# The opening's w_ada product in column halves with its own ring slots, and the convolution's first gated rows rounded early

## The reference, cut to what matters

```python
mod = silu(c) @ w_ada + b_ada            # 9 vectors of 1024: shift, scale, gate of three places
sh1, sc1, gt1, ... = split(mod, 9)
u = rmsnorm(x, g_norm_ffn1) * (1 + sc1) + sh1
h = x + 0.5 * gt1 * (silu(u @ w_in[:, :2816]) * (u @ w_in[:, 2816:])) @ w_out
...                                      # attention and pooling, a second FFN, a last rmsnorm
b_gate, c_gate, h = split(x @ conv_w_in, 3)
y = (b_gate * causal_dwconv3(c_gate * h)) @ conv_w_out
x = layer_norm(ALPHA * x + y)
x = layer_norm(ALPHA * x + top-2-of-64-experts(x))      # expert weights: 3 MB each, all are loaded
...                                      # sparse attention, a second set of 64 experts
```

## Time and profile before

| | us |
|---|---|
| median of 3 runs | 2670.45 |
| lowest, highest | 2669.17, 2670.98 |
| profiled execution | 2668.95 |
| its span | 2667.0 |

### The profile page before, as it was taken

How to read it: one execution, slowest core, us unless ns; L and a number is a source line. 1 busy time by engine, 2 the same in 40 slices (tenths; PEclk the granted TensorE clock), 3 DMA queues, 4 the chain that set the end, 5 groups by cost and what they waited for, 6 DMA issues and landing times.

```text
span 2667.0 us, 38184 instructions
## 1 busy us (share of the span) xinstructions
PE 2425.0 (91%) x14539; PEld 1778.1 (67%) x14540; DVE 1352.8 (51%) x2767; ACT 860.5 (32%) x1484; POOL 215.5 (8%) x168
## 2 busy tenths in 40 slices
PE   6999999999999999999987888889989988888787
PEld 4888888877678888787754444447755865544454
DVE  5766645442552244544653444336955574444445
ACT  4222335565332224322322111124367341211122
POOL 1000003000000000000011111110036001111110
PEclk9999999999999999999999898899999989989899
DMA  8666422112432232222489999995220349999987
GB/s 287 212 196 196 165 87 89 63 49 79 142 111 95 94 118 101 81 95 95 171 359 422 422 422 422 422 401 193 80 95 21 145 195 421 422 422 422 422 336 303
DMA packets 201771, 591.62 MB, mean 222 GB/s; under 512 B 10512, under 2 KB 126432, under 8 KB 152784
## 3 DMA queue, kind: packets, MB, share of 16 engines
q1 hardware_dynamic: 198496, 575.47, 56.1%
q0 software_dynamic: 2896, 14.47, 1.7%
q10 hardware_dynamic: 288, 0.43, 0.1%
HBM read 588.17 MB, written 7.41 MB: 223 GB/s over the span
## 4 chain that ended last, share of the span: by engine, by line
PE 66%; DMA 22%; DVE 4%; ACT 3%; issue 2%; SPq 1%; POOL 1%; DVEq 0%; ACTq 0%; POOLq 0%
PE bank L2181 40%; DMA arena<-in_exp_w 19%; PE bank L2550 7%; PE bank L2274 5%; DMA ring<-in_exp_w 2%; PE bank L2573 1%; SPq L609 1%; PE bank L2438 1%; DMA ring<-in_w_ffn_in 1%; DVE ring_low L1351 1%; PE bank L2785 1%; PE bank L2361 1%; PE bank L2591 1%; PE bank L2519 1%; PE bank L2754 1%
## 5 line engine op out<-in xcount | busy, mean ns | idle before, releaser
L2181 PE MATMUL bank<-parts 128*128 128x512 f32 x2560 | 795.9, 392 | 10.9 <-DVE parts L1628 4.8
L2181 PEld LDWEIGHTS bank<-parts 128*128 128x128 f32 x2560 | 482.2, 189 | 112.4 <-DVE ring_low L1351 6.5
L2181 PE MATMUL bank<-parts,ring_low 128*128 128x512 f32 x1280 | 500.5, 391 | 0.0
L2550 PE MATMUL bank<-ring,arena 128*32 128x256 f32 x2112 | 303.8, 447 | 83.6 <-DMA arena<-in_exp_w 83.6
L1351 DVE TENSOR_TENSOR ring_low<-ring,parts 128x2048 fp32r<-128x2048 f32 x109 | 245.1, 2251 | 179.2 <-ACT parts L838 170.2
L2550 PE MATMUL bank<-arena 128*32 128x256 f32 x2112 | 304.0, 447 | 32.2 <-issue 25.5
L838 ACT ACTIVATE parts<-ring 128x2048 fp32r<-128x2048 f32 x109 | 204.4, 1879 | 227.7 <-DMA ring<-in_w_ffn_in 115.4
L2181 PEld LDWEIGHTS bank<-parts,ring_low 128*128 128x128 f32 x1280 | 241.8, 189 | 51.0
L765 POOL COPY arena<-U 128x2048 f32<-128x2048 f32 x60 | 112.6, 1907 | 1762.5 <-PE bank L2550 1043.9
L2550 PEld LDWEIGHTS bank<-ring,arena 128*32 128x32 f32 x2112 | 141.0, 124 | 158.5 <-issue 135.0
L2550 PEld LDWEIGHTS bank<-arena 128*32 128x32 f32 x2112 | 142.1, 124 | 82.8 <-issue 49.1
(11 more groups left out here) (380 smaller groups left out, 3587.8 us busy)
## 6 DMA issues: line engine op xcount, KB each, us to landing
ring<-in_exp_w SPq DMA_DIRECT2D x188, 1024.0 KB, 18.9
arena<-in_exp_w SPq DMA_DIRECT2D x132, 1024.0 KB, 18.6
U<-in_exp_w SPq DMA_DIRECT2D x60, 1024.0 KB, 23.1
ring<-in_w_ffn_in SPq DMA_DIRECT2D x44, 1024.0 KB, 5.6
ring<-in_w_ada SPq DMA_DIRECT2D x36, 1024.0 KB, 5.5
ring<-in_w_ffn_out SPq DMA_DIRECT2D x20, 1024.0 KB, 5.1
ring<-in_w_in SPq DMA_DIRECT2D x18, 1024.0 KB, 5.0
ring<-in_conv_w_in SPq DMA_DIRECT2D x12, 1024.0 KB, 5.1
```

The source lines that it names most:

```text
L2181: i = mm(o, a[:, cols[0], cols[1]], b, start=first_ and n == 0, stop=last_ and n == 2)
L2550: x = mm(bank[p][lanes_at:lanes_at + LANES, 0:2 * P].rearrange("p (w n) -> p w n", w=2), XW[:, k, LANES * (2 * p + e):LANES * (2 * p + e) ...
```

## The change

**Opening.** The eight w_ada chunks are cut as 512 rows by 512 columns, in the order scale and shift of columns 0 to 511, then scale and shift of 512 to 1023. Each group of two chunks gives half a vector. Only four chunks are loaded ahead of the first pair of FFN chunks, which has ring slots 4 and 5 for itself; the other four come behind it, then two more w_ada chunks, then the second pair (slots 2 and 3). VectorE, not ScalarE, copies the turned tiles of x. The first pair's chunks are split in two parts each (rows of tiles 0 to 3 and 4 to 7), and tiles 0 to 3 are made while the second half of the shift and scale is not yet known. `first_pair` multiplies A's two halves of the columns with tiles 0 to 3, then w_ada chunks 4 and 5, B's first half of the columns, chunks 6 and 7, B's second half, and then tiles 4 to 7. The turn of the layer norm's vectors moves behind the pair.

**Convolution.** `EARLY` is a pair of memories for the rounded first four row tiles. Its high part lies in `parts` 8192 to 10240 and its low part at 10240 to 12288, which is where `W13[0]` takes expert 0. The roundings of row tile d - 2 stand in steps 2 to 5, the output product reads its first chunk from there, and expert 0's W1 and W3 are loaded after the third use count of `conv_out`. The waits of TensorE for the end of the convolution move to the second half of the columns.

```diff
+        EARLY = (rounded(8192, 4, SEQ), rounded(10240, 4, SEQ))
...
-            return first["ffn0"] + (0 if c == 0 else 5 + 4 * (c - 1))
+            return first["ffn0"] + (0 if c == 0 else 8 if c == 1 else 5 + 4 * c)
...
-                    stream_a.append((flat(A["w_ada"], 2 * (a % 4), 2, D * (1 - a // 4), D), 2, D, "ada_mm", a + 1))
+                    stream_a.append((flat(A["w_ada"], 4 * (a % 2), 4, D * (1 - a // 2 % 2) + 512 * (a // 4), 512), 4, 512,
+                                     "ada_mm", a + 1))
...
-        ada_chunks(ADA_FIRST)
+        ada_chunks(4)
...
-                    ada_chunks(3 if c in (0, 10) else 2)
+                    ada_chunks({0: 6, 1: 3, 10: 3}.get(c, 2))
...
+            if n < ffn_at(0, 2):
+                return (0, 1, 2, 3, 4, 5, 0, 1, 2, 3, 0, 1, 2, 3, 0, 4, 5)[n]
             if n < first["mix"]:
-                return n % RING
+                return (n - ffn_at(0, 2)) % RING
...
-                sp.wait_ge(*((sem("ffn1_out_used"), 12), (sem("att_max"), ATT["max"] + 64))[layer])
-                for j in range(2):
-                    matrix(layer, j, 0, 0)
+                if layer:
+                    sp.wait_ge(sem("att_max"), ATT["max"] + 64)
+                    for j in range(2):
+                        matrix(layer, j, 0, 0)
...
                 for j in range(2):
                     matrix(layer, j, 3, 3)
+                if layer == 0:
+                    sp.wait_ge(sem("conv_out_used"), 3)
+                    for j in range(2):
+                        matrix(layer, j, 0, 0)
...
+                row(1)
+                first_high(0, 0)
+                act.wait_ge(sem("ada_mod"), 4)
+                tile(0)
+                tile(1)
+                first_high(1, 0)
+                tile(2)
+                tile(3)
+                first_high(0, 1)
+                first_high(1, 1)
+                row(2)
+                row(3)
+                act.wait_ge(sem("ada_mod"), ADA_FIRST)
+                for k in range(4, KT):
+                    tile(k)
...
+                if 2 <= d < 6:
+                    act.wait_ge(sem("conv_bc"), d - 1)
+                    tile_high(EARLY[0][:, d - 2], BC[:, d - 2])
...
+            dve.wait_ge(sem("ada_mm"), 2)
+            nc.vector.tensor_copy(AROW[:, 0], bank[4][:]).then_inc(sem("ada_row"), 1)
+            vector(0)
+            for k in range(KT):
+                dve.wait_ge(sem("x_tp"), k + 1)
+                nc.vector.tensor_copy(H[:, k], bank[k % 4][:]).then_inc(sem("x_h"), 1)
+                if k == 6:
+                    dve.wait_ge(sem("keep"), 16)
+                    roots(0)
+            dve.wait_ge(sem("x_h"), KT)
+            dve.wait_ge(sem("rstd"), 1)
+            normed(0)
+            vector(1)
+            first_low(0, 0)
+            rest_of(0)
+            normed(1)
+            rest_of(1)
+            normed(2)
+            first_low(1, 0)
+            rest_of(2)
+            normed(3)
+            rest_of(3)
+            first_low(0, 1)
+            first_low(1, 1)
+            vector(2)
+            for k in range(4, KT):
+                normed(k)
+            vector(3)
+            for k in range(4, KT):
+                rest_of(k)
             ffn(0)
...
+                if 2 <= d < 6:
+                    tile_low(tiles_at["conv_out"] + d - 2, EARLY, d - 2, BC[:, d - 2])
...
+            def first_pair():
+
+                def product(which, s, k):
+                    return passes(bank[2 * s + which][:], both(which), (k, slice(P * s, P * s + P)),
+                                  (UP[0][:, k], UP[1][:, k]), k == 0, k == KT - 1)
+
+                pe.wait_ge(sem("opening"), 2)
+                for k in range(4):
+                    pe.wait_ge(sem("t_low"), tiles_at["ffn0"] + k + 1)
+                    for s in range(2):
+                        product(0, s, k)
+                ada_rows(4)
+                ada_rows(5)
+                pe.wait_ge(sem("opening"), 3)
+                for k in range(4):
+                    product(1, 0, k)
+                    if k == 1:
+                        ada_sums(2)
+                ada_rows(6)
+                ada_rows(7)
+                for k in range(4):
+                    product(1, 1, k)
+                    if k == 1:
+                        ada_sums(3)
+                pe.wait_ge(sem("w_low"), 2)
+                for s in range(2):
+                    for k in range(4, KT):
+                        pe.wait_ge(sem("t_low"), tiles_at["ffn0"] + k + 1)
+                        for which in range(2):
+                            x = product(which, s, k)
...
+                    src = EARLY if name == "conv_out" and c == 0 else x
...
+                    if name == "conv_out" and (half, c) == (1, 0):
+                        pe.wait_ge(sem("conv_bc"), 8)
+                        pe.wait_ge(sem("side_out"), 9)
...
-            pe.wait_ge(sem("conv_bc"), 8)
-            pe.wait_ge(sem("side_out"), 9)
+            pe.wait_ge(sem("conv_bc"), 7)
+            pe.wait_ge(sem("conv_cg"), 8)
```

More of the change, by code:

```diff
@@ L400, in build @@
         first["ada"] = 0
-        ada_first = tuple(range(ADA_FIRST))
+        ada_first = tuple(a if a < 4 else a + 2 for a in range(ADA_FIRST))
         def ada_chunks(n):
@@ L903, in norm, with first_high, first_norm, row @@
                     tile_high(UM[0][:, KT - 1], U[:, KT - 1])
+            def first_high(i, part):
+                which, n = splits[i]
+                landed(act, which, n)
+                C = slice(CHUNK // 2 * part, CHUNK // 2 * part + CHUNK // 2)
+                made = A_(high(i)[0][:, C], ring[:, slots[which][n], C], ACT.Copy)
+                if part == 0:
+                    st.did(made)
+                else:
+                    made.then_inc(sem("w_high"), 1)
+            def first_norm():
+                act.wait_ge(sem("pool_step"), 4)
+                st.wait()
+                A_(small[:, 56:57], epsc[:, 0:1], ACT.Sqrt)
+                A_(small[:, 48:52], small[:, 60:64], ACT.Sqrt, scale=1.0 / D, bias=epsc[:, 0:1]).then_inc(sem("root"), 1)
+                def row(g):
+                    act.wait_ge(sem("ada_mm"), 2 * g + 2)
+                    if g >= 2:
+                        act.wait_ge(sem("ada_sum"), g - 1)
+                    evac(AROW[:, g % 2], bank[4 + g % 2][:], "ada_row")
+                def tile(k):
+                    act.wait_ge(sem("normed"), k + 1)
+                    A_(UP[0][:, k], U[:, k], ACT.Identity, bias=mod[:, k:k + 1]).then_inc(sem("t_high"), 1)
+                row(1)
[13 more added lines that the diff above has]
+                    tile(k)
             def ffn(i):
@@ L1600, in _ @@
             st.wait()
[L1601 to L1620, removed]
+            nc.vector.tensor_copy(CZ[:, :, 0:1], csil[:].unsqueeze(2)).then_inc(sem("opening"), 1)
+            def vector(g):
+                dve.wait_ge(sem("ada_sum"), g + 1)
+                c = KT * (1 - g % 2) + 4 * (g // 2)
+                TTn(mod[:, c:c + 4], bank[7][:, 4 * g:4 * g + 4], par[:, PC["b_ada"] + c:PC["b_ada"] + c + 4], ALU.add)\
+                    .then_inc(sem("ada_mod"), 2)
+                dve.wait_ge(sem("ada_mod"), 2 * g + 2)
+                if g % 2 == 0:
+                    C = slice(2 * g, 2 * g + 4)
+                    seq(STT(out=gains[:, C], in0=mod[:, c:c + 4], scalar=1.0, in1=par[:, PC["g_ffn1"] + 2 * g:PC["g_ffn1"] + 2 * g + 4],
+                            op0=ALU.add, op1=ALU.mult))
@@ L1621, in _, with first_low, normed @@
+            def first_low(i, part):
+                dve.wait_ge(*((sem("act_step"), TT + i + 1), (sem("w_high"), i + 1))[part])
+                n = slots["a"][splits[i][1]]
+                C = slice(CHUNK // 2 * part, CHUNK // 2 * part + CHUNK // 2)
+                TTn(ring_low[:, n, C], ring[:, n, C], high(i)[0][:, C].bitcast(F32), ALU.subtract)\
+                    .then_inc(sem(("opening", "w_low")[part]), 1)
+            def normed(k):
                 STT(out=U[:, k], in0=H[:, k], scalar=gains[:, k:k + 1], in1=bank[6][:],
@@ L1622, in _, with rest_of @@
                     op0=ALU.mult, op1=ALU.mult).then_inc(sem("normed"), 1)
[L1623 to L1626, removed]
+            def rest_of(k):
                 dve.wait_ge(sem("t_high"), tiles_at["ffn0"] + k + 1)
@@ L2156, in _ @@
             pe.wait_ge(sem("csil"), 1)
-            pe.wait_ge(sem("ada_cz"), 1)
+            pe.wait_ge(sem("opening"), 1)
             ada_rows(0)
             ada_rows(1)
+            ada_sums(0)
             pe.wait_ge(sem("x_in"), 16)
@@ L2193, in pair @@
                             pe.wait_ge(g, c * 2 + (base + s - 1))
-                        if s == 0 and it is None and r == 0 and i:
+                        if s == 0 and it is None and r == 0:
                             pe.wait_ge(sem("w_low"), s0 + 2)
                         if it is None and r == s == 0:
[L2197 to L2200, removed]
```

(6 more changed lines are left out.)

71 lines of the change are left out of this document (27 added, 44 removed).

## The result

| | before | after |
|---|---|---|
| median us (20 runs each, same chip) | 2667.39 | 2672.22 |
| lowest, highest | 2665.23, 2671.5 | 2668.32, 2674.68 |
| profiled execution, its span | 2668.95, 2667.0 | 2669.14, 2667.3 |

The ratio is 1.0016, with a 95% interval of 1.001 to 1.0022. The change makes the kernel 4.8 us slower, where 5.5 us faster was forecast. The difference lies under the 0.2% that the prediction took for the bound of what can be told, but 20 runs on each side resolve it.

What follows compares the result with a forecast made beforehand. It took TensorE, busy 91% of the span, as the bound, and VectorE's serial list as the opening's new one. Join 5.3 plus opening 0.2 gave 5.5 us: 2670.45 - 5.5 = 2664.9 us, range 2660.5 to 2668.5.

Steps and rivals of the forecast that it cites:

- the opening: Start of the kernel through the first FFN pairs: earlier TensorE start, later a new wait; 0.2 us won in all.
- the wait at 92 us: TensorE's wait of 1.2 us in the opening before; forecast to go because the second pair's chunks are loaded early.
- the join: Convolution's end to its output product: TensorE's 3.83 us without work goes, with the clock price behind it; 5.3 us won.
- the steps of the convolution: Steps 2 to 5, which take the moved roundings: cost 0, at worst 0.2 us for two tight steps.
- Rival (2): At the join, another wait replaces the roundings (second chunk or step 5): 2 to 3 us won, 2667 to 2668; chance 0.12.
- The matrices: First expert's two matrices (2 MiB), loaded later: cost 0, or 5.0 us if they stood in the path.
- Rival (3): The matrices reach the experts' first turn late because transfers share bandwidth; the 5.3 us are lost again, 2670; chance 0.08.
- The opening, up to TensorE's start: Kernel start to the first pair's first matrix product: TensorE starts at 28.4 us, 40.88 before.
- From there: Opening behind TensorE's start: VectorE's list delays the second B; with the wait at 92 us and clock, 0.2 us won.
- VectorE's list: Serial w_ada, low-part and gate work in the opening: starts at 49.7 us, takes 19.9, becomes the new bound.
- second B: First pair's second B in the opening: TensorE waits 5.5 us until 69.6, then loses 1.45 us to the clock.
- Rival (4): Opening: clock falls in TensorE's broken groups from 28 to 36 us and stays low; 3.0 us slower, 2673.5; chance 0.07.

Runs made afterwards that it cites:

- e1: The whole change with the first FFN's ring slots renamed from s to (s + 5) mod 6, nothing else: 2666.58 us, ratio 0.9994 to the kernel before.
- e2: The kernel before with the first FFN's ring slots turned from n mod 6 to (n + 1) mod 6, nothing else: 2676.49 us, ratio 1.0035.
- e3: The kernel before with only the convolution's part of the change (early roundings, later load of expert 0's matrices): 2662.65 us, ratio 0.9982.
- e5: e1 with VectorE doing the second B's low part and gate product ahead of w_ada chunk 10: 2659.57 us, ratio 0.9966 to the kernel before.
- e4: e1 without the convolution's part, so the opening alone with renamed slots: 2670.38 us, ratio 1.0011 to the kernel before.
- e6: e5 with GpSimd's small loads waiting for the eighth A chunk's use, not the second: 2657.6 us, ratio 0.9966 to the kernel before.
- e7: e1 with GpSimd's small loads waiting for the eighth A chunk's use, VectorE's order unchanged: 2666.31 us, ratio 0.999 to the kernel before.

## Why the prediction was wrong

**The step that failed** is a term that the prediction put at nothing without a reason: the stretch between the opening, whose account ends with the wait at 92 us, and the join at 1258.5. It says that a microsecond at either place is one of the whole, so it took all between as unchanged. The prediction read the new slots only where they help (the first pair's own slots, the second pair loaded early) and summed the opening up to the first FFN's steady part. But the rotation of the slots goes on to the end of the FFN, and what it hands over there decides when the next stage's first load may start. This put 8.5 us into the path (wait 10.0 instead of 1.7), and e1 and e2 show it. The prediction's own range, 2660.5 to 2668.5, had no room for it: no rival looked past 100 us on the opening's side. Beside the 8.5 us the terms missed by little: against the forecast the opening lost 1.6 us more, the way from the mixing product to the convolution's last step 1.2 us, and the join with what follows it won 0.8 us more. Together this is 10.4 us, from 5.5 won to 4.9 lost. The time of 2664.9 was in addition counted from the three runs of 2670.45, 3.1 us above the 20 runs of the same kernel.

**The join** was right: 5.3 us forecast, 5.7 measured, in after and in e3. The gap of 3.83 us is gone, and the clock behind it is 1.00 where it was 0.59. The price behind the gap was 1.8 us, not 1.45: the first 144 matmuls of the product take 32.70 us instead of 34.54. With the steps of the convolution this is a little less. Each of the two steps where VectorE's part stands ahead of the low parts costs 0.3 us in the step that follows (it takes 16.59 against 16.38, and starts 0.1 later), 0.6 together; the forecast said 0, at worst 0.2. Rival (2) had named the place, but its price of 2 to 3 us is not there.

**The matrices** cost nothing by waiting. The first turn's products have no wait for a transfer, in after or in e3. Transfers ran for longer, as worked out: between 1338 and 1344 us, where nothing moved, 421 GB/s now move, and they end near 1347, which is the forecast 1341.6 with the shift of 5.3. Rival (3) falls. The first turn's first product did get slower, 6.18 us against 5.25 and 6.12 in e3, at a granted clock of 0.59 for its 6.18 us, where it was 0.72 for the 5.41 us before. The wait for transfers behind the turns takes that up (22.56 us in after, 23.60 before).

**The opening, up to TensorE's start**: 28.4 forecast (its terms add up to 28.5), 28.49 measured. The A chunk was there at 25.15, not at 25.7, and the split and the first tile behind it took about as much longer, so the two misses cancel.

**From there** the mechanism was right and three sizes were off. VectorE's list started at 50.77, not at 49.7: TensorE was through the last sums at 46.85 instead of 46.0, and from there to the list it took 3.9 us and not 3.7. The list itself was 0.4 shorter than 19.9 us, so TensorE's second B came at 70.32, not 69.6. TensorE itself was ready for it at 65.7, not at 64.1, so the wait was 4.60 us and not 5.5. The clock cost 2.3 us and not 1.45: the 1032 matmuls from 70.32 take 236.96 us, and at the 0.2274 of the earlier trace rows they would take 234.6. The prediction took the price that it had read behind a gap of 3.8 us, itself too low, for a gap that it expected to be 5.5. With 0.2 lost at the second B, 2.3 of clock and 1.2 won at 92 us, 1.3 us are lost, where 0.2 won were forecast. The Trainium skill ("TensorE: Matmul & The Clock Gate", Part 1), by which an idle TensorE falls to half its clock, spoke against this part. The trace agrees, with 0.53 for 5.5 us behind the gap. e5 shows that all of this loss hung on one place in VectorE's order.

**Rival (4)** described a clock that falls in the broken groups. It did fall, to 0.54 between 28.49 and 35, but it came back within these groups and VectorE's list had only 1.07 us of delay from all causes, not the 5.5 from which the rival decides. Its time of 2673.5 lies near the median by accident: e1 has the same opening, and 2666.58.

## What to carry to other kernels

When the order of loads in a ring changes, follow the rotation to the end of the stretch and compare, for the first load of the next stage, which chunk it waits for: one changed index, without an instruction more, made e2 9 us slower. Where an engine works off a serial list, put what another engine waits for ahead of what nobody waits for yet, before making its start earlier: the order in e5 brought 7 us, the 12 us earlier start alone lost 2 to 3 in e4. What that order would bring to the kernel before, without the earlier start, was not run. And add up such a change at several landmarks of the chain and not only where it is made: a local sum of -5.5 us had the sign wrong.

## What the runs showed that was not expected

**Equal code, other clock.** Between the mixing stage's first product and the convolution's start the code of these kernels is the same. The stretch takes 708.2 us in before and e2, 708.6 in after, 708.7 in e6, 709.8 in e5, 710.0 in e3, 710.6 in e4, 711.1 in e1 and 711.2 in e7. The difference is, for the most part, in how long the granted clock stays at its lower level, above all at the start of the stretch. The first window is before, the second e1, each from the start of the mixing product (columns as rows 6):

```profile
413.39:416.70 3.31, 3.31 (x8) 2.68 (x9) 3.31 (x6) 3.31 (x7) 0.00 (x0) 0.52 0.03 7
```

```profile
415.06:420.60 5.54, 5.54 (x13) 4.46 (x14) 5.54 (x7) 5.54 (x11) 0.00 (x0) 0.50 0.02 4
```

Both follow a wait of 1.7 us. The product's 64 matmuls take 15.61 us in the one and 16.85 in the other, and 15.93 in after, whose wait was six times as long. So the length of the wait does not decide. The place in the program alone does not either: in e3 the product starts at 413.46, 0.07 us from before, and takes 16.43. And the clock did not fall in this wait, which begins at 411.7 in before, but ahead of it: the eight small matmuls between 409 and the wait run at 0.63 in before, and at 0.50 in e3. In before the clock is back by 417, in e3 not by 418. The two windows of before, then those of e3:

```profile
409.00:411.80 2.80, 2.04 (x8) 1.75 (x8) 1.11 (x6) 1.87 (x2) 2.07 (x7) 0.63 0.88 355
...
417.00:418.00 1.00, 1.00 (x6) 0.90 (x5) 1.00 (x2) 1.00 (x3) 0.00 (x0) 1.00 0.00 0
```

```profile
409.00:411.80 2.80, 2.07 (x8) 1.78 (x8) 1.05 (x5) 1.92 (x2) 1.79 (x6) 0.50 0.96 392
...
416.50:418.00 1.50, 1.50 (x5) 1.15 (x4) 1.50 (x3) 1.50 (x4) 0.00 (x0) 0.50 0.00 0
```

This is where e1's gain of 8.5 us lost a part: 1.2 us in this product. What sets it was not settled: there is one trace of each kernel. For a reader of profiles it means that 1 to 3 us between two traces can come from unchanged code, so the small shifts in the table above are not by themselves effects of an edit.

**The first groups.** At the first pair's start the clock was at half in after and in e1. But e1 had 18 matmuls from 28.49 to 35.00 at 0.76 where after had 16 at 0.54, and e1 was not ahead at the second B (70.33 against 70.32). Here a slower TensorE cost nothing that the traces show, since it has to wait for the tiles of this group anyway: the fourth tile's low part ends at 35.2 in after.
